# Four gathers in flight at most: a wait for an earlier landing before each expert-row gather

## What is computed

```python
s = jnp.einsum('thjd,hjkd->thjk', q, sub_keys)      # 8 heads, 2 x 128 sub-keys
sv, si = lax.top_k(s, 16)                           # then top 16 of the 16 x 16 sums
eidx = i1 * 128 + i2                                # 8 x 16 = 128 experts of 16384 for each token
u, v = expert_u[eidx], expert_v[eidx]               # rows of 1024 float32
act = gelu(einsum('td,thkd->thk', xb, u))
y = einsum('thk,thkd->td', g * act, v)
```

## Time and profile before

| | |
|---|---|
| time, median of 3 runs | 2734.98 us (2733.08 to 2751.05) |
| the profiled execution | 2735.33 us |
| its span, first to last instruction | 2733.5 us |
| mean granted TensorE clock | 0.903 |

### The profile page before, as it was taken

The page is one execution under the profiler, slowest core; times in us unless marked ns, Lnnn a source line. Parts: engine busy times, 40 slices in busy tenths (PEclk is TensorE's granted clock), DMA queues, the critical chain, the costliest instruction groups (busy, mean ns, idle before and its releaser), DMA issues.

```text
span 2733.5 us, 32507 instructions
## 1 busy us (share of the span) xinstructions
PE 2266.0 (83%) x12206; PEld 1754.0 (64%) x12206; DVE 1539.3 (56%) x3643; ACT 691.5 (25%) x2067; POOL 1051.8 (38%) x1060
## 2 busy tenths in 40 slices
PE   8999959988659998898996346598667899997898
PEld 8999859887648887787541225234356455545785
DVE  3441367845999998765227869410265657573110
ACT  7661336612235555200110100210012000001220
POOL 0000031333446663444567655565533446470000
PEclk9999979998879999999998758799876899998899
DMA  6556659998969998999899798899896899996175
GB/s 245 217 193 254 250 206 352 396 393 320 388 263 389 391 406 309 348 414 381 329 411 353 260 370 347 320 358 343 314 353 232 320 385 359 355 413 226 66 277 211
DMA packets 186092, 869.30 MB, mean 318 GB/s; under 512 B 20800, under 2 KB 21056, under 8 KB 153680
## 3 DMA queue, kind: packets, MB, share of 16 engines
q0 software_dynamic: 147456, 536.94, 51.2%
q1 hardware_dynamic: 37904, 328.20, 30.9%
q10 hardware_dynamic: 576, 2.10, 0.2%
HBM read 865.06 MB, written 2.10 MB: 317 GB/s over the span
## 4 chain that ended last, share of the span: by engine, by line
PE 64%; DVE 17%; issue 7%; ACT 5%; another core or an unknown queue 4%; DMA 2%; DVEq 0%; SPq 0%; ACTq 0%
PE ps L888 63%; DVE rows L2170 4%; DVE ps L2190 1%; DMA scan<-in_wq 1%; DVE tmpx L1815 1%; DVE h L2190 1%; DMA wr<-in_wso 1%; ACT junk L1324 1%; DVE si L1735 1%; ACT ynT L1500 0%; PE ps L1221 0%; ACT L1295 0%; DVE ci L1735 0%; DVE wb L2048 0%
## 5 line engine op out<-in xcount | busy, mean ns | idle before, releaser
L861 POOL DMA_INDIRECT rows<-in_pu,eidx x512 | 485.3, 948 | 629.7 <-DVE dots L2170 480.1
L2170 DVE CUSTOM_DVE_ANT_0 rows<-rows,ps 128x1024 f32<-128x1024 f32 x512 | 595.0, 1216 | 6.7 <-issue 6.1
L888 PE MATMUL ps<-uT,wr 128*128 128x128 f32 (+2 forms) x3456 | 553.6, 318 | 23.3 <-issue 14.2
L888 PEld LDWEIGHTS ps<-uT,wr 128*128 128x128 f32 x3456 | 504.7, 196 | 56.7 <-issue 24.2
L888 PE MATMUL ps<-hT,wr 128*128 128x384 f32 (+2 forms) x1536 | 373.3, 401 | 73.0 <-issue 52.1
L888 PEld LDWEIGHTS ps<-hT,wr 128*128 128x128 f32 x1536 | 256.9, 200 | 187.6 <-issue 90.9
L861 POOL DMA_INDIRECT rows<-in_pv,eidx x256 | 289.1, 1129 | 212.7 <-DVE h L2190 98.4
L861 POOL DMA_INDIRECT rows<-in_pv,eidxT x256 | 240.7, 940 | 179.5 <-issue 67.4
L888 PE MATMUL ps<-rows,wz 128*32 128x512 f32 x1024 | 217.2, 637 | 33.7 <-DMA rows<-in_pv,eidxT 19.5
L2190 DVE SCALAR_TENSOR_TENSOR ps<-rows,wgt,ps 128x1024 f32<-128x1024 f32 x126 | 161.8, 1284 | 10.4 <-DMA rows<-in_pv,eidx 7.7
L2190 DVE SCALAR_TENSOR_TENSOR h<-rows,wgt,h 128x1024 f32<-128x1024 f32 x128 | 163.8, 1280 | 6.6 <-DMA rows<-in_pv,eidx 5.4
(11 more groups left out here) (408 smaller groups left out, 2990.9 us busy)
## 6 DMA issues: line engine op xcount, KB each, us to landing
wr<-in_wg SPq DMA_DIRECT2D x48, 1536.0 KB
wr<-in_wsc SPq DMA_DIRECT2D x24, 1536.0 KB
wr<-in_wso SPq DMA_DIRECT2D x24, 1536.0 KB
wr<-in_wgu SPq DMA_DIRECT2D x33, 1024.0 KB
wr<-in_wgate SPq DMA_DIRECT2D x24, 1024.0 KB
wr<-in_wqku SPq DMA_DIRECT2D x15, 1024.0 KB
wr<-in_wo SPq DMA_DIRECT2D x12, 1024.0 KB
wr<-in_wdn SPq DMA_DIRECT2D x8, 1536.0 KB
```

Of the source, the lines that this page charges most:

```text
L861: e.indirect_dma_start(ring[i % NR], None, A[table], bass.IndirectOffsetOnAxis(ap=index[:, t, k:k + 1], axis=0)).then_inc(gathered[i % NR] ...
L888: return e.matmul(o, l, r, start=start, stop=stop, skip_group_check=True)
L2170: e.tensor_tensor_reduce(row, row, wide[:], 1.0, 0.0, MUL, ADD, dots[:, k:k + 1]).then_inc(*dve.up(*u))
```

## The change

A constant `FLIGHT = 4` is added, and in `gather()` job `i` waits for the landing of job `i - 4` too. The semaphore of that job's buffer has to reach 16 times the number of landings up to and with it. Nothing else changes: order of units, buffers, users, the wait for job `i - 13`.

```diff
 NW = 3
 NR = 13
+FLIGHT = 4
...
                 if i >= NR:
                     old = jobs[i - NR]
                     w.wait_ge(*(pe.at("rows", *old[1:3], old[3] // 2) if old[0] == "row" else dve.at(*old)))
+                if i >= FLIGHT:
+                    w.wait_ge(gathered[(i - FLIGHT) % NR], 16 * ((i - FLIGHT) // NR + 1))
                 e.indirect_dma_start(ring[i % NR], None, A[table],
                                      bass.IndirectOffsetOnAxis(ap=index[:, t, k:k + 1], axis=0)
                                      ).then_inc(gathered[i % NR], 16)
```

## The result

| comparison made together | before, median | changed, median | ratio |
|---|---|---|---|
| first, the one forecast | 2734.03 us (4 runs) | 2781.48 us (2768.41 to 2789.43, 4 runs) | 1.0161 [1.0094, 1.0228] |
| again, on kind II (below) | 2581.26 us (15 runs) | 2777.13 us (2767.33 to 2779.56, 4 runs) | 1.0728 [1.0679, 1.0778] |

What follows compares the result with a forecast made beforehand. TensorE (83% busy) and DVE (56%) were taken to bound the kernel, gathers mattering only where one waits for rows or POOL is late. Terms 5 + 1 + 1 + 10 = 17 us gave 2752 us, +0.6%, range 2728 to 2790.

Steps and rivals of the forecast that it cites:

- never binds: Rival: the cap of four never binds where it counts, 2735 us (2730 to 2740); chance 0.24.
- I take 1.4 us: Clean stretches: pace from one gather to the next with four in flight, 1.4 us against 1.275.
- upper bound of 1.69: Upper bound of the pace with four in flight, 1.69 us, from the full queue's 6.74 us from issue to landing.
- 1.5 us where DVE sums rows: Pace taken where DVE sums rows: POOL's longer issue adds 0.05 us, and landing times are less regular.
- the term 10: Exposed end of tile 3, 2368 to 2472 us: last sum +14.4 us, less 4 us of cover; +10 us, upper bound about +21.
- +5 at 1355 to 1440: Rows of tile 1 on TensorE between query products: 58 gathers at 1.4 us plus weights, +5 us, bounds 0 and +24.
- +1 at 1734 to 1855: 79 gathers in 121 us, 1.53 us each, so 1.4 fits: +1 us, +13 at a pace of 1.69.
- +1 to 1944: Exposed end of tile 2, 1904 to 1944 us: a 3.36 us pause pays for the cap, +1 us, +8 at 1.69.
- The other stretches stay at nothing: Remaining stretches: 0 us, since up to nine landed rows wait in buffers, some 11 us of DVE's work.
- 0 at 2265 to 2330: 44 gathers get 9 to 20 us later, but POOL's following 27.9 us idle with a full ring hides it: 0 us.
- weights land sooner: Rival: shorter gather queues shorten weight waits at 550 to 760 us, -26 us if half go, 2709 us; chance 0.12.
- the cliff: Rival: latency doesn't shrink with a shorter queue, pace 1.69 us, +66 us, 2801 us (2775 to 2810); chance 0.14.

Runs made afterwards that it cites:

- experiment 1: Changed kernel with FLIGHT = 12 instead of 4, so the wait holds no gather back: 2580.82 us beside 2580.89 us before, ratio 0.9997.
- experiment 7: Changed kernel with the cap of four only for i >= 896, the v rows of tile 3: 2602.86 us, ratio 1.0088 to before.
- experiment 8: Changed kernel with the cap of four only for i < 256, the rows of tile 0: 2610.11 us, ratio 1.0101 to before.

## Why the prediction was right or wrong

The range (2728 to 2790) and the side were right; the forecast of +17 us was a third of the 47 us measured, and that it lies in the range is luck, because two large errors have opposite signs. The loss is 196 us on kind II, and before had 153 us of slowness on the first chip (2734 against 2581 us) that four in flight take away almost whole: the changed kernel is only 4 us slower there. 196 - 153 + 4 = 47.

- *"So five or six are in flight in steady flow, and a cap of four does bind."* Right, and it excluded the likeliest error: the rival "never binds" (and with it the estimate of 3.2 us that the Trainium skill's page "DMA: Bandwidth & Descriptors", section "Anatomy of one DMA — SWDGE (gpsimd) path", leads to) is out by the 1.67 us pace. The chain of waits now holds 33% DMA, against 2% before. The number was too small where weights share the DMA engines: by the packet records before's landings take a median of 10.0 us at 1355 to 1440 us and 11.0 us at 2368 to 2471 us, six to seven gathers in flight.
- *The wait instruction at nothing.* Right (experiment 1, 0.9997).
- *"I take 1.4 us".* This is the step of the first two exposed stretches that failed. The formula (round / 4) was right; the round was read from TensorE's side, 5.56 us from a gather's start to the matmul that takes it. POOL is the one that waits now, and it starts 0.7 us later after a landing than a consumer does. The round is 6.3 to 6.7 us, the pace 1.675 us. The upper bound of 1.69, taken from the full queue's 6.74 us, hit the pace, for a reason that was not mine: the queueing shrank (the medians of 10.0 and 11.0 us became 5.8 and 6.5 us) and POOL's reaction took its place.
- *1.5 us where DVE sums rows.* It was 51 gathers in 103 us with weights between (2368 to 2471), 2.0 us each; of that a round of 6.5 + 1.1 us makes 1.9. The last sum was to be 14.4 us later and was 39.3; less the cover of 4 us that is the 35 us of lag at 2515 us, of which 2 were there at 2414. The place, the cover and the idle TensorE behind it were right, the term 10 was 33.
- *+5 at 1355 to 1440.* 33 us on kind I, above the bound of 24. Part of it may be what the forecast named at L882 and priced at nothing: the products of tile 2 start at 1481.46 instead of 1442.17, and DVE, which had 4.2 us of cover, now waits 10.51 us for them. No run takes this apart from the rows.

```profile
1481.46 5.49 POOL L885 TENSOR_TENSOR oh<-oh,sif 128x256 f32<-128x256 f32 x8
1486.98 2.29 DVE L2020 TENSOR_REDUCE cx<-oh 128x128 f32<-128x2048 f32 x1 [10.51 <-POOL oh L885]
```

- *+1 at 1734 to 1855, +1 to 1944.* "1.53 each; 1.4 fits" turns with the pace: at 1.675 it doesn't fit. From 1762 to 1939 us the lag grows by 21 us, all of the two bounds (13 + 8). And the pause of 3.36 us that was to pay for the exposed end was no full ring. The gather at 1927.50 is job 759, its buffer is that of job 746, and TensorE was through with that one at the latest when the first group below ends, at 1918.06 us, while POOL stood idle from 1924.14 on. The profile names no releaser for the pause.

```profile
1911.04 7.02 PE L888 MATMUL ps<-rows,wz 128*32 128x512 f32 x24 [3.30 <-issue]
1918.73 1.91 PE L888 MATMUL ps<-rows,wz 128*32 128x512 f32 x8 [0.67 <-DMA rows<-in_pv,eidxT]
```

- *"The other stretches stay at nothing because 13 row buffers lie between a gather and its use."* Wrong for the u rows of tile 2, which the forecast didn't price. VectorE sums them in the same queue as the pieces of attention and pooling (tiles `up` and `lf`) that TensorE waits for. On kind II the lag grows by 25 us from 1480 to 1680 us of before. In that stretch (1556 to 1781 us with four) VectorE waits 33.5 us for these rows instead of 10.1, and TensorE waits for `up` 69.9 us instead of 54.8 and for `lf` 27.4 instead of 19.1. On kind II 21 us more come from 2050 to 2220 us, where TensorE waits 16.1 us for `fT`, another tile of VectorE's, and not at all in before; experiment 7, which caps the v rows of tile 3 alone, doesn't have them, so they go with rows that are late before these. No run caps the u rows of tile 2 or 3 alone.
- *0 at 2265 to 2330, hidden by 27.9 us of full ring.* Right: 32 gathers for 44, the lag stays between +1 and +2 us from 2240 to 2414 us, and the cover is used up (experiment 7).
- *"Before 1300 us nothing should move."* Wrong twice. The v rows of tile 0 from 893 to 1044 us cost 24 us (16 to 29 us in experiment 8), since I priced 550 to 760 us, where the cap hardly binds, and didn't look at the next consumers. And -17.6 us came before that, from slow stretches of TensorE that I had read past: the list of waits put 116.2 us of TensorE's idle time (L888) under "issue", with no releaser, and I counted it as given.
- *The rival "weights land sooner".* No: in 550 to 760 us TensorE's waits for weights are longer than before, 27.2 us for `in_wq` instead of 22.5, and on kind II the lag stays at 3.5 us there. There is something that makes the kernel faster, but another: the gaps that vanish on kind I.
- *The chances.* 0.27 for slower by over 1% was too little. With a round of 6.5 us, the 13 + 8 + 21 + 24 = 66 us of the cliff would have been the main case.

## What to carry to other kernels

A cap of N transfers in flight gives a pace of one round over N, and the round includes the time in which the *issuing* engine notices the landing (here 5.3 + 1.1 us), not that of the consumer; if the stretch runs at nearly the DMA engines' rate, price the cap from the longest round that the trace shows, and look at every stretch in which rows are consumed, early ones too. Idle time of the bounding engine that the profile puts down to "issue" is not a constant of the kernel: find out what runs beside it before taking it as given, and look whether a semaphore was waited for all the same. When a kernel's time differs by 5% from chip to chip, measure a change on both kinds of chip: here the same five in flight is 0.8% faster on one and 1.4% slower on the other.

## What the hardware showed that I had not expected

- Chips, or their condition at the time, differ by 5.4 to 5.9% for the same kernel: before took 2721 to 2734 us in four comparisons and 2581 us in two. The kernel with four in flight took 2781 and 2777 us.
- On kind I TensorE falls to one matmul in a multiple of about 0.70 us (1.42 and 2.13 us in the rows above) while bursts of gathers are under way, 7.5 us of idle time in the first burst with 13 gathers, 2.4 with six, 0.6 with five and none with four.
- POOL starts its next gather 1.1 us after the last packet of the one that it waits for; DVE starts 0.4 us after.
- A gather of 512 KB with nothing else under way has its last packet 3.9 to 4.0 us after its start; as one of four, a median of 5.3 us.
